# A two-layer sparse and forgetting attention trunk on one core: loads ordered by need, forget sums and function tables ahead of attention, the last two output units in halves of positions

## The chip, the cores and the metric

The kernel runs on one core of one Trainium2 chip. The metric is device time in microseconds (us) of one execution. All times come from runs on the chip, all stretches from one profiled execution.

## What is computed

The reference is a trunk of two layers over 512 positions of width 1024, in float32:

```
for l in range(DEPTH):                      # DEPTH = 2
    h = rms_norm(x, norm_g[l])
    proj = jnp.einsum('btd,dc->btc', h, w_in[l])
    q_a, kv_a, g_a, z_a, q_b, k_b, v_b, f_b, z_b, merge = jnp.split(proj, split_at, axis=-1)
    y_a = nsa_mixer(q_a, kv_a, g_a, cmp_pe_k[l], cmp_w1_k[l], cmp_w2_k[l],
                    cmp_pe_v[l], cmp_w1_v[l], cmp_w2_v[l], cos, sin) * jax.nn.silu(z_a)
    y_b = fox_mixer(q_b, k_b, v_b, f_b, b_forget[l]) * jax.nn.silu(z_b)
    r_a, r_b = jnp.split(merge, 2, axis=-1)
    merged = (jax.nn.sigmoid(r_a) * (y_a @ w_proj_nsa[l]) + jax.nn.sigmoid(r_b) * (y_b @ w_proj_fox[l]))
    x = x + merged @ w_out[l]
return rms_norm(x, final_g)
```

`nsa_mixer` has 16 heads in two groups. It compresses blocks of 32 keys and values (adds position vectors, a hidden layer with weights w1, silu, a second layer w2), attends to the compressed, the selected and the windowed keys with rotated queries and keys, and weighs the three by gates. `fox_mixer` is causal attention with a bias from the running sum over positions of log_sigmoid(f + b_forget), the forget sums.

## The kernel before

The program is written out engine by engine, with semaphores between them. Activations stand transposed: 1024 features as eight chunks of 128 partitions by 512 positions. Every projection is cut into *units* of 128 output columns. A unit is one load of weights (512 KB, `load` on SyncE's queue, into one of two buffers `w_raw`), a rounding into `w_hi` by ScalarE (`split_hi`), a rest `w_lo` by VectorE (`split_lo`), and 24 matmuls of 512 columns on TensorE (`unit_piece`, L1545: three for each of eight chunks). A load waits until `w_lo_done` says that its buffer has been split for the unit two before.

A layer has five stages.

- Prologue (first layer only): TensorE multiplies a constant tile 12 and 8 times (`run_in`), turns the eight chunks of x, ScalarE and VectorE copy them out and make `u_hi` and `u_lo`, and unit 0 follows chunk by chunk.
- Ten units of keys and values, `kv(0)` to `kv(9)`: 0 and 1 are the inputs of the compression (`c_raw`), 2 and 3 the gates and forget logits (narrow, 48 and 16 columns, multiplied together as `gf_w` on L1725 and L1726), the others keys, the first queries and values. Between them come `hidden(a)` (the compression's hidden layer for keys, a = 0, and values, a = 1), the rotation on GpSimd, the forget sums on VectorE (L1401, L1404, L1407, with an exponential and a logarithm on ScalarE), and turns of v.
- Eight cycles of attention, in which further units are spread between the steps of a `Plan`. Before the first one VectorE finishes `v_rest` and `z_silu_of`, and ScalarE `z_tanh_of`.
- The merge, and eight output units (`U_OUT`) with the residual sum.
- After the last layer: turns of the normed output, sums of squares, a root, a scaling by row and four stores of 512 KB.

What matters for the order: each engine runs its instructions strictly in the order in which they are written. Unit 4 uses the same accumulator `acc[0]` as unit 0, and may start once `c_raw` of unit 0 has been read, which VectorE does after `split_lo(*kv(4))`:

```
split_lo(*kv(4))
dve.wait_ge(rstd_spread, l + 1)
dve.tensor_copy(rstd[:, :], misc[:, :]).then_inc(rstd_done, 1)
dve.wait_ge(rstd_done, l + 1)
c_raw_of(0)
```

Of the kernel before, what the change touches and what calls it, by code (L numbers as in the profile page):

```python
# [143 lines left out]
def bass_trunk(nc, x, norm_g, w_in, b_forget, pe_k, w1_k, w2_k, pe_v, w1_v, w2_v, w_nsa, w_fox,  # L144
               w_out, final_g, rope_c, rope_s, out):
    ctx = ExitStack()
    with ctx:
# [177 lines left out]
        c_landed = sem("c_landed")  # L325
# [49 lines left out]
        o_t_done = sem("o_t_done")  # L375
        o_turned = sem("o_turned")
# [75 lines left out]
        def _(sp):  # L452
# [7 lines left out]
            def load_compression(l, n):  # L460

                for a, w1, w2, pe in ((0, w1_k, w2_k, pe_k), (1, w1_v, w2_v, pe_v))[n:n + 1]:
                    for j in (slice(0, CJ // 2), slice(CJ // 2, CJ)):
                        sp.dma_start(c_w1[:, a:a + 1, j, :],  # L464
                                     w1.rearrange("l (j p) h -> p l j h", p=P)[:, bass.ds(l, 1), j]
                                     ).then_inc(c_landed, 16)
                    sp.dma_start(c_w2[:, a:a + 1, :],
                                 w2.rearrange("l h d -> h l d")[:, bass.ds(l, 1)]).then_inc(c_landed, 16)
                    with nc.allow_non_contiguous_dma(reason="8 kB of position vectors, transposed"):
                        for par in range(2):  # L470
                            sp.dma_start(c_pe[HD * par:HD * par + HD, a:a + 1, :],
                                         pe.rearrange("l (j a) d -> a d l j", a=2)[par][:, bass.ds(l, 1)]
                                         ).then_inc(c_landed, 16)
# [41 lines left out]
            for qt in range(QT):  # L515
                sp.wait_ge(o_scaled[qt % 2], qt // 2 + 1)
                sp.dma_start(out[0, qt * P:(qt + 1) * P, :], o_nat[:, qt, :]).then_inc(o_stored, 16)
# [4 lines left out]
        def _(pool):  # L522
# [135 lines left out]
            pool.wait_ge(rope_landed, 32)  # L658
            for l in range(DEPTH):
# [8 lines left out]
                            0.0).then_inc(pads, 1)  # L668
                rotate(l, 0, q_raw)
# [28 lines left out]
        def _(act):  # L698
# [91 lines left out]
            def body(cycle):  # L790
# [55 lines left out]

                m = nsa.m
# [24 lines left out]
            table_of_sqrt()  # L872
            for to, src in ((cosT[:, :], rope_c), (sinT[:, :], rope_s)):
# [5 lines left out]
            split_hi(0, 0, wait=False)  # L879
            act.wait_ge(gains_done, 1)  # L880
            for k in range(KT):
                if k % 2:
                    act.wait_ge(x_turned, k + 1)
                    act.activation(xT[:, k, :], x_banks[k % 4][:, :], ACT.Copy).then_inc(x_odd, 1)
                    act.wait_ge(x_odd, k // 2 + 1)
                else:
                    act.wait_ge(x_done, k // 2 + 1)
                u_high(0, k)
# [6 lines left out]
            for l in range(DEPTH):  # L895
# [55 lines left out]
                q_round((0, 1), [(rope_done, l * 10 + 2)])  # L951
                act.wait_ge(f_exp, 3 * l + 1)
                act.activation(f_b[F_ROWS, :], f_b[F_ROWS, :], ACT.Ln, bias=1.0).then_inc(f_exp, 1)
                split_hi(*kv(8))
# [3 lines left out]
                act.wait_ge(f_step, 6 * l + 5)  # L958
                act.activation(f_hi[F_ROWS, :], f_b[F_ROWS, :], ACT.Copy).then_inc(f_exp, 1)
# [61 lines left out]
                for k in range(KT):  # L1021
                    if k < KT - 1 or l + 1 < DEPTH:
# [808 lines left out]
```

## Time and profile before

| | us |
|---|---|
| median of 3 runs | 1512.32 (1512.21 to 1512.59) |
| the profiled execution | 1511.46 |
| its span, first to last record | 1509.7 |
| TensorE matmuls busy | 1477.7 |
| VectorE, ScalarE, GpSimd busy | 1027.5, 906.2, 482.9 |
| mean granted clock of TensorE | 0.993 of full |

The profiled time is the span and 1.76 us around it, and lies 0.86 us under the median. TensorE is busy 98% of the span, so time can come only from where it stands idle or runs at its lower clock: between the start and the first cycle of each layer, and at the end.

### The profile page before, as it was taken

To read this page: it belongs to the slowest core of one execution; us is meant where nothing else is said; L and a number is where in the kernel's file an instruction comes from. 1 tells how busy PE (TensorE), PEld (TensorE's weight loads), DVE (VectorE), ACT (ScalarE), POOL (GpSimd) and SP (SyncE) were. 2 spreads that over 40 slices of the span, in tenths; PEclk is the share of its full clock that TensorE was granted. 3 is DMA by queue.
4 is the path that set the end of the run, shared out by engine and by line. 5 is a ranking of instruction groups with operands and counts; after the bars stand their busy time and mean duration, and the time that the engine had idled before them with its cause. 6 is when DMAs were issued, how large, how long until landed. Compare 5 with 4: busy or idle time off the path is not lost.

```text
span 1509.7 us, 24892 instructions
## 1 busy us (share of the span) xinstructions
PE 1477.7 (98%) x7645; PEld 1241.2 (82%) x7645; DVE 1027.5 (68%) x2455; ACT 906.2 (60%) x1883; POOL 482.9 (32%) x578
## 2 busy tenths in 40 slices
PE   7999999999999999999999999999999999999997
PEld 6878888888888888888877888888888888888886
DVE  4778788788788874434557788788788787643443
ACT  4667777777777762223445777777777776422233
POOL 1425445445455420000013445445355363000000
PEclk9999999999999999999999999999999999999999
DMA  9222222222122143332452212122222221433332
GB/s 247 69 73 57 56 57 56 56 53 61 46 52 62 51 125 98 93 102 84 127 148 73 67 47 61 51 57 57 57 57 56 56 57 47 149 89 106 86 96 84
DMA packets 221827, 117.86 MB, mean 78 GB/s; under 512 B 17560, under 2 KB 220336, under 8 KB 221232
## 3 DMA queue, kind: packets, MB, share of 16 engines
q1 hardware_dynamic: 219584, 107.66, 26.9%
q0 software_dynamic: 1728, 8.66, 1.6%
q8 instruction: 40, 0.66, 0.2%
q10 hardware_dynamic: 432, 0.54, 0.1%
q14 instruction: 43, 0.35, 0.1%
HBM read 110.41 MB, written 6.42 MB: 77 GB/s over the span
## 4 chain that ended last, share of the span: by engine, by line
PE 85%; DVE 6%; ACT 3%; issue 2%; POOL 1%; SPq 1%; DMA 1%; ACTq 0%; DVEq 0%; POOLq 0%
PE acc L1545 60%; PE o_pair L1623 7%; PE turned L1605 7%; PE scores L1597 4%; PE scores L1596 4%; ACT w_hi L704 1%; DVE w_lo L1044 1%; PE misc L1634 1%; DMA w_raw<-in_w_in_dram 1%; DVE kk_lo L1146 1%; DVE yt_lo L1429 1%; SPq L464 1%; PE misc L1568 1%; PE o_pair L1649 0%; PE scores L1679 0%
## 5 line engine op out<-in xcount | busy, mean ns | idle before, releaser
L1545 PE MATMUL acc<-u_hi,w_hi 128*128 128x512 f32 x1120 | 444.9, 397 | 11.5 <-DVE c_raw L1085 9.5
L1545 PE MATMUL acc<-u_lo,w_hi 128*128 128x512 f32 x1120 | 442.9, 395 | 0.0
L1545 PE MATMUL acc<-u_hi,w_lo 128*128 128x512 f32 x1120 | 442.7, 395 | 0.0
L820 ACT ACTIVATE prob<-prob,row_max 128x128 f32<-128x128 f32 (+3 forms) x384 | 215.1, 560 | 184.6 <-DVE row_max L1210 182.7
L1044 DVE TENSOR_TENSOR w_lo<-w_raw,w_hi 128x1024 fp32r<-128x1024 f32 x188 | 233.0, 1240 | 96.4 <-ACT w_hi L704 94.4
L631 POOL TENSOR_SCALAR prob<-prob,row_inv,gates 128x128 f32<-128x128 f32 (+3 forms) x256 | 169.9, 664 | 336.5 <-DVE row_inv L1217 332.4
L704 ACT ACTIVATE w_hi<-w_raw 128x1024 fp32r<-128x1024 f32 x188 | 197.9, 1053 | 104.9 <-PE acc L1545 86.6
L1545 PEld LDWEIGHTS acc<-u_hi,w_hi 128*128 128x128 f32 x1120 | 211.5, 189 | 54.5 <-issue 12.0
L1545 PEld LDWEIGHTS acc<-u_hi,w_lo 128*128 128x128 f32 x1120 | 211.6, 189 | 40.0
L1545 PEld LDWEIGHTS acc<-u_lo,w_hi 128*128 128x128 f32 x1120 | 211.6, 189 | 38.1
L1210 DVE CUSTOM_DVE_ANT_0 prob<-scores,causal 128x128 f32<-128x128 f32 (+3 forms) x384 | 184.9, 482 | 43.5 <-PE scores L1597 33.2
L829 ACT ACTIVATE pt_hi<-turned 128x128 fp32r<-128x128 f32 (+3 forms) x384 | 163.3, 425 | 44.8 <-PE turned L1605 42.8
L1222 DVE TENSOR_TENSOR pt_lo<-turned,pt_hi 128x128 fp32r<-128x128 f32 (+3 forms) x384 | 186.3, 485 | 3.4 <-ACT pt_hi L829 3.0
L628 POOL TENSOR_SCALAR prob<-prob,row_inv 128x128 f32<-128x128 f32 (+3 forms) x128 | 145.3, 1137 | 85.3 <-DVE row_inv L1217 84.9
L1605 PE MATMUL turned<-ident,prob 128*128 128x128 f32 x960 | 169.7, 275 | 2.9 <-POOL prob L628 1.1
L1605 PEld LDWEIGHTS turned<-ident,prob 128*128 128x128 f32 x960 | 117.1, 141 | 31.3 <-POOL prob L631 3.5
L1217 DVE RECIPROCAL row_inv<-row_sum 128x1 f32<-128x1 f32 x384 | 60.4, 157 | 76.5 <-ACT prob L820 73.5
L1596 PE MATMUL scores<-kk_hi,q_nsa 128*128 128x128 f32 (+3 forms) x256 | 100.4, 393 | 3.0 <-DVE row_max L1210 3.0
L1545 PE MATMUL acc<-yt_hi,w_hi 128*128 128x512 f32 x256 | 101.0, 395 | 0.6 <-DVE w_lo L1044 0.6
L1545 PE MATMUL acc<-yt_hi,w_lo 128*128 128x512 f32 x256 | 100.4, 392 | 0.0
L1545 PE MATMUL acc<-yt_lo,w_hi 128*128 128x512 f32 x256 | 99.5, 389 | 0.0
L1597 PE MATMUL scores<-kk_lo,q_nsa 128*128 128x128 f32 (+3 forms) x256 | 82.1, 321 | 0.0
(197 smaller groups left out, 2228.8 us busy)
## 6 DMA issues: line engine op xcount, KB each, us to landing
w_raw<-in_w_in_dram SPq DMA_DIRECT2D x140, 512.0 KB, 3.8
w_raw<-in_w_proj_nsa_dram SPq DMA_DIRECT2D x16, 512.0 KB, 3.9
w_raw<-in_w_proj_fox_dram SPq DMA_DIRECT2D x16, 512.0 KB, 4.1
w_raw<-in_w_out_dram SPq DMA_DIRECT2D x16, 512.0 KB, 4.1
x_scratch<-xT POOLq DMA_DIRECT2D x2, 2048.0 KB, 7.8
xT<-x_scratch POOLq DMA_DIRECT2D x2, 2048.0 KB, 8.6
x_nat<-in_x_dram SPq DMA_DIRECT2D x4, 512.0 KB, 8.1
c_w<-in_cmp_w_k_dram SPq DMA_DIRECT2D x4, 512.0 KB, 7.5
```

The lines of the kernel that those rows point to most:

```text
L628: ins = pool.tensor_scalar(p, p, row_inv[:, ring:ring + 1], None, ALU.mult)
L631: ins = pool.tensor_scalar(p, p, row_inv[:, ring:ring + 1], gate, ALU.mult, ALU.mult)
L704: act.activation(w_hi[:, par, :, 0:width], w_raw[:, par, :, 0:width], ACT.Copy).then_inc(w_hi_done, 1)
L820: act.activation(prob[:, ring, 0:width], prob[:, ring, 0:width], ACT.Exp, bias=row_max[:, ring:ring + 1], scale=-1.0, accum_out=row_sum[:, ...
L829: act.activation(pt_tiles(pt_hi, a, qt), turned_tiles(s, qt), ACT.Copy)\
L1044: dve.tensor_tensor(w_lo[:, par, :, 0:width], w_raw[:, par, :, 0:width], w_hi[:, par, :, 0:width], ALU.subtract).then_inc(w_lo_done, 1)
L1210: dve.tensor_tensor_reduce(prob[:, ring, 0:width], scores[s % 2][:, 0:width], causal[:, T - width:T], -SCALE, BIG, ALU.add, ALU.min, row_m ...
L1222: dve.tensor_tensor(pt_tiles(pt_lo, a, qt), turned_tiles(s, qt), pt_tiles(pt_hi, a, qt), ALU.subtract).then_inc(pt_lo_done, 1)
L1545: ins = pe.matmul(acc[par][0:width, :], w[:, par, k, 0:width], rhs, start=(n == 0), stop=(n == 23))
L1596: pe.matmul(to, q_hi, k_hi[:, 0:n], start=True, stop=False)
L1597: pe.matmul(to, q_with, k_lo[:, 0:n], start=False, stop=True).then_inc(s_mm, 1)
L1605: ins = pe.transpose(turned[s % 2][:, P * kt:P * kt + P], prob[:, s % SM_RING, P * kt:P * kt + P], ident[:, :])
```

## The change

Five things change.

- *Loads.* The compression's loads are cut in two (`load_hidden` for w1, `load_second` for w2 and the position vectors) with a semaphore for keys and one for values. Those for keys go behind units 2 and 3, those for values behind unit 5.
- *Prologue.* `run_in` does 8 and 4 times. ScalarE copies the odd chunk first and then makes `u_hi` of both, TensorE takes unit 0 by pairs of chunks, and ScalarE issues the loads of the rotation tables and biases behind the chunks.
- *Forget sums.* The logarithm goes ahead of the rounding of q on ScalarE, and the sums ahead of `q_rest` on VectorE.
- *Tables.* One element of Tanh is computed ahead of `v_round`, and `z_tanh_of`, `z_silu_of` and the second `v_rest` go into steps 1, 3 and 0 of the first cycle.
- *End.* Output units 6 and 7 are computed for positions 0 to 255 and then for 256 to 511, with squares, root, turn, scaling and stores by halves. The last of the four stores is issued by ScalarE.

```diff
+            def load_hidden(l, a, w1):
+                for j in (slice(0, CJ // 2), slice(CJ // 2, CJ)):
+                    sp.dma_start(c_w1[:, a:a + 1, j, :],
+                                 w1.rearrange("l (j p) h -> p l j h", p=P)[:, bass.ds(l, 1), j]
+                                 ).then_inc(c_landed[a], 16)
...
-                    if n in (1, 3):
-                        load_compression(l, n // 2)
+                    if n == 2:
+                        load_hidden(l, 0, w1_k)
+                    if n == 3:
+                        load_second(l, 0, w2_k, pe_k)
+                    if n == 5:
+                        load_hidden(l, 1, w1_v)
+                        load_second(l, 1, w2_v, pe_v)
...
+            for k in range(0, KT, 2):
+                act.wait_ge(x_turned, k + 2)
+                act.activation(xT[:, k + 1, :], x_banks[(k + 1) % 4][:, :], ACT.Copy).then_inc(x_odd, 1)
+                act.wait_ge(x_done, k // 2 + 1)
+                u_high(0, k)
+                act.wait_ge(x_odd, k // 2 + 1)
+                u_high(0, k + 1)
             for to, src in ((cosT[:, :], rope_c), (sinT[:, :], rope_s)):
                 act.dma_start(to, src).then_inc(rope_landed, 16)
...
+                act.wait_ge(z_done, 2 * PAIRS * l + 1)
+                act.activation(z_th[:, 0:1], ones[:, 0:1], ACT.Tanh)
                 act.wait_ge(x_saved, 16 * (l + 1))
                 v_round(l * 10, v_pair[:, :, 0, :, 0:HD])
                 v_round(l * 10 + 1, v_pair[:, :, 1, :, 0:HD])
-                z_tanh_of(2 * PAIRS * l, 0)
...
+                if cycle.first:
+                    at(0, lambda: v_rest(l * 10 + 1, v_pair[:, :, 1, :, HD:2 * HD], v_pair[:, :, 1, :, 0:HD]))
+                    at(3, lambda: z_silu_of(2 * PAIRS * l, 0))
...
+            last_piece(0, 0)
+            turn_out(KT - 4)
+            last_piece(0, 1)
+            turn_out(KT - 3)
+            last_piece(1, 0, 0, 14)
+            last_sums(0)
+            last_piece(1, 0, 14)
+            last_turns(0)
+            last_piece(1, 1)
+            last_sums(1)
+            last_turns(1)
```

SyncE's queue at the start of the program, before; `c_w` and `c_pe` are the compression's weights and position vectors, 128x8x128 of `w_raw` a full unit, 128x8x48 and 128x8x16 the narrow units 2 and 3:

```order
L457 DMA w_raw<-in_w_in_dram 128x8x128
L464 DMA c_w<-in_cmp_w_k_dram 128x8x128 x2
L467 DMA c_w<-in_cmp_w_k_dram 128x64
L471 DMA c_pe<-in_cmp_pe_k_dram 64x16x1 x2
L457 DMA w_raw<-in_w_in_dram 128x8x48
L457 DMA w_raw<-in_w_in_dram 128x8x16
L464 DMA c_w<-in_cmp_w_v_dram 128x8x128 x2
L467 DMA c_w<-in_cmp_w_v_dram 128x64
L471 DMA c_pe<-in_cmp_pe_v_dram 64x16x1 x2
L457 DMA w_raw<-in_w_in_dram 128x8x128 x6
```

The same queue with the change:

```order
L466 DMA w_raw<-in_w_in_dram 128x8x128
L466 DMA w_raw<-in_w_in_dram 128x8x48
L472 DMA c_w<-in_cmp_w_k_dram 128x8x128 x2
L466 DMA w_raw<-in_w_in_dram 128x8x16
L478 DMA c_w<-in_cmp_w_k_dram 128x64
L482 DMA c_pe<-in_cmp_pe_k_dram 64x16x1 x2
L466 DMA w_raw<-in_w_in_dram 128x8x128 x2
L472 DMA c_w<-in_cmp_w_v_dram 128x8x128 x2
L478 DMA c_w<-in_cmp_w_v_dram 128x64
L482 DMA c_pe<-in_cmp_pe_v_dram 64x16x1 x2
L466 DMA w_raw<-in_w_in_dram 128x8x128 x4
```

Between unit 3's load and unit 4's there stood the five loads for values; now there stand three small ones for keys, and the two halves of the keys' w1 stand ahead of unit 3's load.

VectorE before the first cycle, before, from the rest of the queries (L1121) to the first row maximum:

```order
L1121 TENSOR_TENSOR q_nsa<-q_rope,q_nsa 64x512 x2
L1085 TENSOR_TENSOR qk_raw<-acc,rstd 128x512
L1044 TENSOR_TENSOR w_lo<-w_raw,w_hi 128x1024
L1388 TENSOR_SCALAR kcb<-scores 64x2x32 x2
L1393 TENSOR_SCALAR vcb<-scores 32x2x64 x4
L1397 SCALAR_TENSOR_TENSOR vcb<-scores,vcb 32x2x64 x4
L1401 SCALAR_TENSOR_TENSOR f_a<-f_a,f_b 32x512
L1404 SCALAR_TENSOR_TENSOR f_b<-ones,f_a 32x512
L1407 TENSOR_SCALAR f_b<-f_b 32x512
L1085 TENSOR_TENSOR z_silu<-acc,rstd 128x512
```

The same place with the change, which begins three rows earlier:

```order
L1435 SCALAR_TENSOR_TENSOR f_a<-f_a,f_b 32x512
L1438 SCALAR_TENSOR_TENSOR f_b<-ones,f_a 32x512
L1441 TENSOR_SCALAR f_b<-f_b 32x512
L1170 TENSOR_TENSOR q_nsa<-q_rope,q_nsa 64x512 x2
L1134 TENSOR_TENSOR qk_raw<-acc,rstd 128x512
L1445 TENSOR_TENSOR f_lo<-f_b,f_hi 32x512
L1093 TENSOR_TENSOR w_lo<-w_raw,w_hi 128x1024
L1452 TENSOR_SCALAR kcb<-scores 64x2x32 x2
L1457 TENSOR_SCALAR vcb<-scores 32x2x64 x4
L1461 SCALAR_TENSOR_TENSOR vcb<-scores,vcb 32x2x64 x4
L1134 TENSOR_TENSOR z_silu<-acc,rstd 128x512
```

The three instructions of the forget sums now stand ahead of the rest of the queries, and their rest `f_lo` ahead of the split of unit 8.

## Rows read from the trace of the kernel before

**Rows 1.** The page, first part: TensorE's busy time, share and instructions.
```profile
PE 1477.7 (98%) x7645; PEld 1241.2 (82%) x7645; DVE 1027.5 (68%) x2455; ACT 906.2 (60%) x1883; POOL 482.9 (32%) x578
```

**Rows 2.** Who TensorE waited for, 0 to 92 us: total, times, longest.
```profile
PE acc L1545 <- DVE c_raw L1085: 6.2, 1, 6.2
...
PE scores L1596 <- DVE row_max L1210: 1.5, 1, 1.5
PE misc L1568 <- DVE z_silu L1085: 1.0, 1, 1.0
```

**Rows 3.** The same, 740 to 850 us; row_max reads as above.
```profile
PE acc L1545 <- DVE c_raw L1085: 3.3, 1, 3.3
...
PE misc L1568 <- DVE z_silu L1085: 0.6, 1, 0.6
```

**Rows 4.** Timeline of TensorE, first layer: start, duration, what, [idle before].
```profile
37.85 0.77 PE L1545 MATMUL acc<-u_hi,w_hi 128*128 128x512 f32 x1 [6.24 <-DVE c_raw L1085]
...
88.02 0.44 PE L1596 MATMUL scores<-kk_hi,q_nsa 128*128 128x384 f32 x1 [1.49 <-DVE row_max L1210]
```

**Rows 5.** Two-us windows of TensorE: length, busy, granted clock, DMA share, GB/s.
```profile
34.00:36.00 2.00, 0.00 (x0) 0.68 0.54 137
...
774.00:776.00 2.00, 0.00 (x0) 0.85 0.00 0
```

**Rows 6.** Timeline of SyncE's queue, first layer.
```profile
20.99 5.12 SPq L464 DMA_DIRECT2D c_w<-in_cmp_w_v_dram  x2
...
29.00 1.37 SPq L457 DMA_DIRECT2D w_raw<-in_w_in_dram  x1
```

**Rows 7.** Timeline of ScalarE and its queue, first layer.
```profile
3.60 0.47 ACTq L877 DMA_DIRECT2D b_f<-in_b_forget_dram  x1
...
18.20 1.04 ACT L704 ACTIVATE w_hi<-w_raw 128x1024 fp32r<-128x1024 f32 x1
...
34.06 1.06 ACT L704 ACTIVATE w_hi<-w_raw 128x1024 fp32r<-128x1024 f32 x1 [6.83 <-DMA w_raw<-in_w_in_dram]
...
63.92 1.27 ACT L743 ACTIVATE q_nsa<-q_rope 64x512 fp32r<-64x512 f32 x2 [4.04 <-POOL q_rope L569]
65.21 1.28 ACT L953 ACT_TABLE_LOAD   x1
...
85.11 1.28 ACT L783 ACT_TABLE_LOAD   x1
```

**Rows 8.** Timeline of VectorE, first layer.
```profile
24.99 0.55 DVE L1314 TENSOR_TENSOR gf_w<-w_raw,gf_w 128x384 fp32r<-128x384 f32 x1
...
35.15 1.23 DVE L1044 TENSOR_TENSOR w_lo<-w_raw,w_hi 128x1024 fp32r<-128x1024 f32 x1 [7.59 <-ACT w_hi L704]
...
72.83 1.38 DVE L1401 SCALAR_TENSOR_TENSOR f_a<-f_a,f_b 32x512 f32<-32x512 f32 x1
...
75.94 0.69 DVE L1085 TENSOR_TENSOR z_silu<-acc,rstd 128x512 f32<-128x512 f32 x1
```

**Rows 9.** The chain that ended last, pieces in order: start, duration, what.
```profile
1.73 5.49 PE scores L1679 x24
...
767.32 5.43 DMA w_raw<-in_w_in_dram
...
776.62 8.36 PE acc L1545 x24
...
841.54 1.22 PE o_pair L1623 x8
...
1492.45 5.51 PE acc L1545 x24
```

**Rows 10.** SyncE's stores at the end, timeline.
```profile
1502.78 2.90 SPq L517 DMA_DIRECT2D out_dram<-o_nat  x4
```

**Rows 11.** DMA, 1503 to 1509.7 us: GB/s in 40 slices.
```profile
GB/s 0 0 0 147 391 416 391 391 391 391 416 391 416 440 367 416 440 391 391 392 391 416 391 416 416 391 391 392 440 465 416 391 416 367 245 0 0 0 0 0
```

More of the change, by code:

```diff
@@ new lines, in last_piece @@
+            def last_piece(h, p):
+                cols = T_HALF[h]
+                act.wait_ge(last_x, 2 * h + p + 1)
+                act.wait_ge(sq_added, (KT - 2) * (DEPTH - 1) + KT - 4 + p)
+                act.activation(squares[:, p, cols], xT[:, KT - 2 + p, cols], ACT.Square).then_inc(last_sq, 1)
+                act.wait_ge(o_turned, KT - 3 + p)
+                act.activation(o_t[:, p, cols], xT[:, KT - 2 + p, cols], ACT.Copy, scale=gain(DEPTH, KT - 2 + p)
+                               ).then_inc(last_o_t, 1)
@@ L1685, in _ @@
                          ).then_inc(gains_turned, 1)
-            run_in(8)
-            for k in range(KT + 4):
+            run_in(4)
+            for k in range(KT + 2):
                 if k < KT:
@@ L1787, in turn_out @@
                     ins.then_inc(o_turned, 1)
-                for k in range(KT):
+                for k in range(KT if l + 1 < DEPTH else KT - 2):
                     unit_piece(0, 24, half0 + U_OUT // 2 + k // 2, k % 2, hi=m_hi, lo=m_lo,
@@ L1794, in _, with last_piece @@
                         turn_out(k - 2)
-            turn_out(KT - 2)
-            sum_squares(DEPTH)
-            turn_out(KT - 1)
+            def last_piece(h, p, first=0, last=24):
+                half, cols = half0 + U_OUT // 2 + KT // 2 - 1, T_HALF[h]
+                for n in range(first, last):
+                    k, which = divmod(n, 3)
+                    if n == 0 and h == 0:
+                        pe.wait_ge(w_lo_done, 2 * half + p + 3)
+                        pe.wait_ge(x_done, X_EVEN + KT * (DEPTH - 1) + KT - 3 + p)
+                    elif n == 0:
+                        pe.wait_ge(last_x, p + 1)
+                    ins = pe.matmul(acc[p][:, cols], (w_lo if which == 2 else w_hi)[:, p, k, :],
+                                    (m_lo if which == 1 else m_hi)[:, k, cols], start=(n == 0), stop=(n == 23))
+                    if n == 23:
+                        ins.then_inc(last_mm, 1)
@@ new lines, in last_sums @@
+            def last_sums(h):
+                pe.wait_ge(last_added, h + 1)
+                pe.wait_ge(var_done, DEPTH + h)
+                for qt in (2 * h, 2 * h + 1):
+                    pe.matmul(misc[:, qt:qt + 1], sq_sum[:, P * qt:P * qt + P], ones[:, 0:1],
+                              start=(qt == 2 * h), stop=False, skip_group_check=True)
+                pe.wait_ge(last_sq, 2 * h + 2)
+                for qt in (2 * h, 2 * h + 1):
+                    ins = pe.matmul(misc[:, qt:qt + 1], squares[:, 1, P * qt:P * qt + P], ones[:, 0:1],
+                                    start=False, stop=(qt == 2 * h + 1), skip_group_check=True)
+                ins.then_inc(last_summed, 1)
@@ new lines, in last_turns @@
+            def last_turns(h):
+                pe.wait_ge(last_o_t, 2 * h + 2)
+                for n in range(2):
+                    qt, bank = 2 * h + n, (scores, turned)[h][n]
+                    if h:
+                        pe.wait_ge(o_copied[n], KT // 2 - 1)
+                    for p in range(2):
+                        ins = pe.transpose(bank[:, P * p:P * p + P], o_t[:, p, P * qt:P * qt + P], ident[:, :])
+                ins.then_inc(last_turned, 1)
+            last_piece(0, 0)
```

206 lines of the change are left out of this document (127 added, 79 removed).

## The prediction, made before the changed kernel ran

> **What bounds the kernel now.** I read the page first. TensorE is busy 98% of the span [rows 1], so a faster VectorE or ScalarE is worth only what TensorE waits for them. Next I read who TensorE waited for, once for each layer's ten units. In the first layer one wait of 6.2 us stands out, for the `c_raw` that frees the accumulator of unit 4; behind it come 1.5 us for the first row maxima and 1.0 us for the value that is turned [rows 2]. The second layer has the same three: 3.3 and 0.6 us [rows 3], and the same 1.5 us for row maxima, in a row that reads like the first layer's [rows 2]. The timeline shows where the long one lies: unit 4 starts at 37.85, so TensorE stopped at 31.6 [rows 4]. Third, the clock. In the window 34 to 36 the granted clock is 0.68, and before and after it stands at one of two levels, full or half (2.4 or 1.2 GHz); 0.68 means 1.28 us at half, so it fell at about 34.7, 3.1 us after the matmuls stopped. In the second layer 0.85 puts the fall at 775.4, 2.1 us after they stopped at 773.3 [rows 3, 5]. The 24 matmuls of unit 4 then took 8.36 us, where a unit at full clock takes 5.51 [rows 9], so the wait costs another 2.85 us there.
>
> Who makes TensorE wait? The load of unit 4 is issued at 29.00, lands for ScalarE at 34.06, and the split on VectorE (35.15), the copy of rstd and the read of `c_raw` lead to 37.85 [rows 4, 6 to 8]. From landing to unit 4 that is 3.8 us. The load's own condition, the split of unit 2 on VectorE, was met at 24.99 + 0.55 = 25.54 [rows 8]. The 3.46 us between are SyncE's issues: from 20.99 it issued the two halves of w1 for values, 5.12 us, and the small loads behind them until 29.00, 2.9 us [rows 6]. In the second layer the same load is issued at 767.32 and needs 5.43 us [rows 9].
>
> **Loads.** With the change only the small loads, 2.9 us, stand between the loads of units 3 and 4. They end near 23.9, and the split at 25.5 decides. If that split keeps its time, unit 4's load goes out 3.46 us earlier and unit 4 starts at 37.85 - 3.46 = 34.4. Transfer kept at the 5.06 us of rows 6 and 7 (29.00 to 34.06). In the second layer up to 5.1 us of issues are gone and 3.3 us of idle can be had; all of it is taken, since the chain only has to move 3.3 us. What is late next: unit 5's load follows directly; the w1 halves for values come out some 7 us later than before, between units 5 and 6. Behind a wait for them on VectorE stand `blocks(1)`, the split of unit 6 and the gates. With 5.12 us of issue from about 28.5 and a landing like unit 4's they are there at about 39, and the work that wants them stands behind the start of unit 4 plus its 5.5 us. So this is free, and starts to cost beyond about 42.
>
> **Prologue.** 24 records of the warm-up took 5.49 us [rows 9], 0.229 each. The first group loses 8 of them, 1.8 us, so the chunks may start up to 1.8 us earlier, if x has landed. Against that ScalarE now issues four loads ahead of the rounding of unit 1, which started at 18.20: one such issue took 0.47 [rows 7], four 1.9 us. Net zero, with bounds -1.8 and +1.9 us.
>
> **The clock.** First layer: idle shrinks from 6.24 to 2.8 us. The falls seen came 3.1 and 2.1 us after the stop, so this gap lies between them. I take half of the 2.85 us as regained, 1.4; bounds 0 and 2.85. Second layer: the gap closes, all 2.85 comes back.
>
> **Forget sums and tables.** On VectorE the sums fill 72.83 to 75.94, 3.1 us [rows 8], ahead of the value that TensorE waited 1.0 us for. In their new place VectorE and ScalarE had a hole: ScalarE waited 4.04 us for the rotated q before L743 [rows 7], and table load and logarithm fit in (1.28 plus an activation). The Tanh table (85.11, 1.28 us [rows 7]), z_tanh and z_silu stood ahead of the first row maximum, for which TensorE waited 1.5 us. VectorE's chain thus moves earlier by 3.5 + 3.1 + at least 1.3 = 7.9 us, more than the 3.5 + 2.5 that TensorE can use at the same clock. So the gain is the waits: 1.5 + 1.0 = 2.5 us in the first layer, 2.1 in the second. Bounds: nothing, if other waits take their place, and the same 2.5 and 2.1, since no more is there. The extra rest, tanh and silu inside the first cycle are three instructions of about 0.7 us; VectorE is busy 68% overall [rows 1], and I cost them at nothing. With no cover they cost up to 2 us a layer.
>
> A rule speaks against this. The row shows a table load of 1.28 us that follows the activation before it at once, since L743 ends at 65.19 and the load starts at 65.21 [rows 7]. The Trainium skill, page "ScalarE: Activation LUTs", section "What ACT_TABLE_LOAD costs", counts some 1.38 us of draining on top, 2.66 us a switch. By that the new Tanh switch ahead of `v_round` would come 1.4 us later a layer, and the sum would be up to 2.8 us less. This trace shows no such drain.
>
> **The end.** Two units by halves: eight matmuls with 2 x (512 + 384 + 256 + 128) = 2560 columns took 1.22 us [rows 9], so one of 256 columns takes 0.122, and 96 of them 11.7 against 2 x 5.51: +0.7. Before, the last unit ended at 1497.96 [rows 9] and the first store was issued at 1502.78 [rows 10], 4.8 us later. The data then flowed at about 400 GB/s from 1503.5 to 1508.8 [rows 11], 5.3 us for 2.1 MB: the four stores are bound by what the transfers carry, not by their issues of 0.73 each. With the change only two stores, 1.05 MB, are left for the end: 2.65 us. TensorE's last piece ends at about 1500.4 (0.7 later for the halves, and an estimated 1.7 for the first half's turns and sums that now stand ahead of it). The rest of the path has half the columns; I take 3.1 of the 4.8 us. Issue at 1503.5, plus 0.73, 2.65 and the 0.9 between the last data and the span's end: 1507.8 against 1509.7, -1.9 us. Bounds: +0.7 if the turns and sums hide nothing, and -3.3.
>
> **The sum.** First layer 3.5 + 1.4 + 2.5 = 7.4, second 3.3 + 2.85 + 2.1 = 8.25, end 1.9: 17.5 us. The span becomes 1492.2, the profiled execution (1.76 around the span) 1493.9, and the median, which lies 0.86 above that execution, 1494.8.
>
> **Rivals.**
> - *All of the clock.* The first layer's gap closes further, because the chunks start earlier and the issues on ScalarE cost less than 1.9 us; then 1.4 to 3.2 us more come back: 1492. For it: the bounds of the prologue. Against: the transfer of 5 us and the 3.8 us behind it stay.
> - *New waits.* In the ten units VectorE is next: with TensorE 3 us earlier at full clock, it waits for `c_blk` ahead of `hidden(0)` or for `w_lo` of unit 8. For it: both layers' VectorE chain has few holes there. Price about 2 to 3 us a layer: 1499.5.
> - *The load comes no earlier.* Unit 4's load is issued at 25.5 but lands near 34, since transfers for x and the tables fill the engines. Then 3.5 + 1.4 and 3.3 + 2.85 are lost, and 6.4 us of gain stay: 1506. Against: the transfers' share was free for some of that time.
> - *The drain of the rule above:* 1497.6.
> - *Slower.* One mechanism: the values' w1, now behind unit 5's load, lands so late that VectorE stands before `blocks(1)`. Its slack is 42 - 39 = 3 us, after which each us costs one. It would have to land beyond 39 + 3 + 17.5 = 59.5 to make the kernel slower; the transfers of rows 6, 7 and 9 took 5 us.
>
> **Chances.** Forecast 60% (1492.5 to 1497), all of the clock 13%, new waits 15%, no earlier load 6%, drain 4%, slower or no change 2%. The range 1490.5 to 1501 leaves out the late load and the last one. Within 0.2%, 3 us, a measurement of this kernel can't tell from no change. Faster 0.97, same 0.02, slower 0.01.
>
> **What would show it.** Right: TensorE's wait for `c_raw` at 3 us or less in the first layer and under 1 in the second; granted clock full from 770 on; the waits for row maxima and z_silu gone from the list; matmuls of 256 columns 0.12 us apart; data of the last stores flowing 2.6 us. Wrong: unit 4's load landing after 32 us, unit 4 of the second layer at 8 us again, new entries `PE <- c_blk` or `PE <- w_lo` of over 1 us, or the first cycle longer than before by the moved tanh and silu.

## The result: 13.0 us faster, of 17.5 forecast

| | median, us | range |
|---|---|---|
| before, on the same chip | 1512.26 | 1512.08 to 1512.59 |
| changed | 1499.26 | 1498.7 to 1500.25 |

Each row is of four runs. The ratio is 0.9917, with a 95% interval of 0.9906 to 0.9929. The forecast was 1494.8 (1490.5 to 1501.0): the direction and the range held. The 4.5 us that are missing bring the time to the number of the rival "new waits", 1499.5. That closeness is in part luck: the new wait costs more in each layer than the rival's 2 to 3 us, and small waits that nobody had counted went away. The profiled execution of the changed kernel took 1498.70 us, its span 1497.0.

The page of the changed kernel, first part, answers to [rows 1]:

```profile
PE 1473.5 (98%) x7677; PEld 1241.3 (83%) x7677; DVE 1029.9 (69%) x2461; ACT 907.5 (61%) x1891; POOL 486.3 (32%) x578
```

TensorE's share has hardly moved, and says nothing here. Who TensorE waited for, changed kernel, 0 to 92 us (total, times, longest), answers to [rows 2]:

```profile
PE acc L1635 <- DVE c_raw L1134: 3.2, 1, 3.2
PE acc L1635 <- DVE w_lo L1093: 2.3, 1, 2.3
PE scores L1769 <- POOL ident L542: 1.7, 1, 1.7
PE acc L1635 <- DVE u_lo L1111: 1.6, 4, 0.7
PE acc L1635 <- issue: 1.2, 1, 1.2
```

The wait for `c_raw` is 3.2 us instead of 6.2, and the waits for row maxima and z_silu are gone. In their place stands one for `w_lo`, of unit 8: one of the entries that the prediction had named as a sign of being wrong. In the second layer it is the only wait that the view lists; it takes the place of [rows 3]. The next view is 740 to 850 us:

```profile
PE acc L1635 <- DVE w_lo L1093: 2.0, 1, 2.0
```

The timeline of TensorE in the first layer (start, duration, what, idle before) answers to [rows 4]:

```profile
35.22 0.47 PE L1635 MATMUL acc<-u_hi,w_hi 128*128 128x512 f32 x1 [3.15 <-DVE c_raw L1134]
...
68.15 0.80 PE L1635 MATMUL acc<-u_hi,w_hi 128*128 128x512 f32 x1 [2.33 <-DVE w_lo L1093]
...
83.63 0.34 PE L1686 MATMUL scores<-kk_hi,q_nsa 128*128 128x384 f32 x1
```

And in windows of 2 us (length, busy, granted clock, DMA share, GB/s), answering to [rows 5]:

```profile
34.00:36.00 2.00, 0.79 (x4) 1.00 1.23 244
...
66.00:68.00 2.00, 0.00 (x0) 0.97 0.00 0
68.00:70.00 2.00, 1.85 (x4) 0.50 0.22 35
70.00:72.00 2.00, 2.00 (x7) 0.67 0.76 227
...
800.00:802.00 2.00, 0.70 (x3) 0.94 0.00 0
802.00:804.00 2.00, 2.00 (x6) 0.50 0.71 173
```

Before unit 4 the clock did not fall in this execution. Before unit 8 it did, in both layers, to half (1.2 GHz); the prediction had wanted it full from 770 us on. The chain of the changed kernel shows the price (start, duration, what), to be read beside a unit at full clock, 5.51 in [rows 9]:

```profile
65.92 2.18 DVE w_lo L1093
68.15 7.23 PE acc L1635 x24
...
799.06 2.19 DVE w_lo L1093
801.30 7.33 PE acc L1635 x24
```

So unit 8 costs 2.3 + 1.7 us in the first layer and 2.0 + 1.8 in the second.

**Where the time went.** The span falls into four sections, bounded by the first score product of 384 columns in each layer and by the begin of the second layer (its sum of squares on TensorE). Each row is worked out from the timelines of one profiled execution, in us:

| kernel | to the first cycle | layer 1 behind it | layer 2 to its first cycle | rest |
|---|---|---|---|---|
| before | 88.02 | 673.28 | 65.92 | 682.48 |
| forecast | 80.6 | 673.3 | 57.7 | 680.6 |
| changed | 83.63 | 673.26 | 59.99 | 680.12 |
| split8_first | 82.08 | 673.37 | 57.10 | 680.25 |
| frest_late | 81.33 | 673.32 | 57.57 | 680.18 |
| forget_back | 83.16 | 673.75 | 59.86 | 680.13 |
| loads_back | 85.12 | 673.30 | 61.95 | 680.23 |
| tables_back | 84.24 | 673.41 | 62.07 | 680.48 |
| prologue_back | 81.21 | 673.26 | 60.10 | 680.13 |
| split8_second_late | 81.28 | 673.27 | 56.72 | 680.13 |
| rope_late | 83.68 | 673.34 | 60.54 | 680.34 |
| end_back | 83.49 | 673.24 | 59.47 | 682.40 |
| loads_alone | 83.75 | 673.34 | 62.03 | 682.38 |
| best2 | 79.80 | 673.18 | 56.71 | 680.21 |
| best2_busy | 79.20 | 673.19 | 56.68 | 680.23 |

The reader sees that the second column does not move: the tanh, silu and rest that went into the first cycle cost nothing. The end gave 2.4 us, 0.5 more than forecast. The first layer gave 4.4 us instead of 7.4, the second 5.9 instead of 8.25. These two sections are what the experiments are about.

### The profile page after: what moved, and what is told of

Same layout as the page of the kernel before. It is cut to its first block, busy times and chain, and to the rows that moved or that the text cites. A ratio compares the mean times of both kernels' runs of the same rounds, so it can differ in the third digit from the quotient of the medians.

```text
span 1497.0 us, 24977 instructions
## 1 busy us (share of the span) xinstructions
PE 1473.5 (98%) x7677; PEld 1241.3 (83%) x7677; DVE 1029.9 (69%) x2461; ACT 907.5 (61%) x1891; POOL 486.3 (32%) x578
## 4 chain that ended last, share of the span: by engine, by line
PE 87%; DVE 5%; ACT 4%; issue 2%; POOL 1%; SPq 1%; DMA 1%; ACTq 0%; DVEq 0%; POOLq 0%
PE acc L1635 61%; PE o_pair L1713 7%; PE turned L1695 7%; PE scores L1687 4%; PE scores L1686 4%; ACT w_hi L720 1%; DVE w_lo L1093 1%; PE misc L1724 1%; PE acc L1896 1%; ACT q_swap L750 1%; DMA w_raw<-in_w_in_dram 1%; DVE yt_lo L1479 1%; PE misc L1658 1%; PE o_pair L1739 0%; PE misc L1732 0%
```

## Experiments

The kernel before was timed again beside the experiments: 1511.79 with the first four, 1511.99 with the next four, 1512.07 with the last four. The changed kernel was not, so that its 1499.26 is compared across 0.2 to 0.5 us of drift. Behind each measured time stands its ratio to the kernel before, with its interval. An interval of a ratio is about 0.0015 to each side, 2.3 us, so differences between two variants of less than that rest on their profiles more than on their medians.

**1. Unit 8's split first.** Both splits of unit 8, and the read of unit 6 that frees its accumulator, go ahead of the forget sums and the rounding of the rotated q.

```diff
                 act.activation(f_b[F_ROWS, :], f_b[F_ROWS, :], ACT.Ln, bias=1.0).then_inc(f_exp, 1)
+                split_hi(*kv(8))
                 q_round((0, 1), [(rope_done, l * 10 + 2)])
...
                 act.activation(f_hi[F_ROWS, :], f_b[F_ROWS, :], ACT.Copy).then_inc(f_exp, 1)
-                split_hi(*kv(8))
...
                 hidden(1)
+                raw_of(*kv(6), l * 10 + 2, [], to=qk_raw)
+                split_lo(*kv(8))
                 dve.wait_ge(f_exp, 3 * l + 2)
...
                 q_rest(l * 26 + 1)
-                raw_of(*kv(6), l * 10 + 2, [], to=qk_raw)
...
-                split_lo(*kv(8))
```

> The changed kernel (1499.3 us), but in both layers the two splits of unit 8 and the read of unit 6 stand ahead of the rounding and the rest of the rotated queries and of the forget sums. Theory A (TensorE now runs ahead of the rotation chain, and unit 8's split, written behind the rotated queries, is the new wait): TensorE's waits for w_lo of 2.3 and 2.0 us fall below 0.5, the stretch at half clock behind them goes, 2.8 + 3.1 us come back: about 1493.5. Theory B (the forget sums' and their rest's new place is the cause, by 2.9 us of extra work ahead of that split): also about 1493.5; the next kernel tells them apart. Theory C (the wait would move to the next unit): within 1 us of 1499.3.

Measured 1493.67 (0.9878, 0.9861 to 0.9894): 5.6 us back, by moving two splits. The wait of unit 8 is gone in both layers (0.3 us stand ahead of unit 9 in the second); clock full from 66 to 74 and from 796 to 804 us. In the second layer the section is 57.10, 0.6 under what I had forecast. The first stays 1.5 above: unit 4 starts at 35.55, not at 34.4, and here the clock fell in its gap. In the changed kernel VectorE's row of this split took 2.17 us, and here (timeline of split8_first) it is:

```profile
62.67 1.23 DVE L1093 TENSOR_TENSOR w_lo<-w_raw,w_hi 128x1024 fp32r<-128x1024 f32 x1 [0.46 <-ACT w_hi L720]
```

**2. Forget sums in their old place.** Logarithm, sums, `f_hi` and `f_lo` as before, all else changed.

```diff
+                q_round((0, 1), [(rope_done, l * 10 + 2)])
                 act.wait_ge(f_exp, 3 * l + 1)
                 act.activation(f_b[F_ROWS, :], f_b[F_ROWS, :], ACT.Ln, bias=1.0).then_inc(f_exp, 1)
-                q_round((0, 1), [(rope_done, l * 10 + 2)])
-                act.wait_ge(f_step, 6 * l + 5)
-                act.activation(f_hi[F_ROWS, :], f_b[F_ROWS, :], ACT.Copy).then_inc(f_exp, 1)
                 split_hi(*kv(8))
...
-                dve.tensor_tensor_scan(f_b[F_ROWS, :], ones[F_ROWS, 0:1].broadcast_to([GF // 2, T]), f_a[F_ROWS, :], 0.0,
...
+                dve.tensor_tensor_scan(f_b[F_ROWS, :], ones[F_ROWS, 0:1].broadcast_to([GF // 2, T]), f_a[F_ROWS, :], 0.0,
...
                 v_of(*kv(7), z_silu[:, 0, :], [])
```

> The changed kernel with the forget sums, their logarithm and their rest back in the old places, all else as changed. Theory A: the split of unit 8 still stands behind the rotated queries and the logarithm; it would end 2.4 us earlier than in the kernel before (69.9), at about 67.5, so TensorE still waits 1.7 to 2 us for it in each layer, and the old wait of 0.5 to 1 us for the values comes back: 1499 to 1502. Theory B: the wait for unit 8 is gone (under 0.5 us) and the time falls by 2 to 5 us, to 1494 to 1497.

Measured 1498.54 (0.9913, 0.9896 to 0.9929), 0.7 below the changed kernel and 0.5 below theory A's range: as the change moves them, with their rests, the sums are worth nothing. The z_silu wait of 1.1 us comes back in each layer. The wait of unit 8 goes in the first layer, where TensorE comes later by the clock that fell at unit 4, and shrinks to 1.5 us in the second; 0.4 us of `w_lo` stand ahead of unit 9 in both, as in the kernel before. What one end gains the other pays. Experiment 6 shows that this is not so of the sums alone.

**3. Loads in their old order.**

```diff
-                    if n == 2:
-                        load_hidden(l, 0, w1_k)
-                    if n == 3:
+                    if n == 1:
+                        load_hidden(l, 0, w1_k)
                         load_second(l, 0, w2_k, pe_k)
-                    if n == 5:
+                    if n == 3:
                         load_hidden(l, 1, w1_v)
                         load_second(l, 1, w2_v, pe_v)
```

> The changed kernel with the compression's loads back behind units 1 and 3, all else as changed. Theory A: unit 4 of the first layer starts near 37.9 again after a wait of some 6 us and at half clock, in the second layer a wait of 3.3 us and half clock, worth 4.3 and 6.2 us; but then the wait for unit 8 (2.8 and 3.1 us) is not there, since TensorE no longer runs ahead: +4.5 us net, 1503 to 1505. If the loads and the wait at unit 8 had nothing to do with each other: +10.5 us, 1510.

Measured 1503.56 (0.9948, 0.9932 to 0.9965), in theory A's range: the loads are worth 4.3 us inside the whole change. The waits for `c_raw` are 6.2 and 3.0 again; the one for unit 8 is gone in the first layer and 0.8 us in the second.

**4. Tables in their old place.**

```diff
-                act.wait_ge(z_done, 2 * PAIRS * l + 1)
-                act.activation(z_th[:, 0:1], ones[:, 0:1], ACT.Tanh)
...
+                z_tanh_of(2 * PAIRS * l, 0)
...
-                    at(0, lambda: v_rest(l * 10 + 1, v_pair[:, :, 1, :, HD:2 * HD], v_pair[:, :, 1, :, 0:HD]))
-                    at(3, lambda: z_silu_of(2 * PAIRS * l, 0))
...
+                v_rest(l * 10 + 1, v_pair[:, :, 1, :, HD:2 * HD], v_pair[:, :, 1, :, 0:HD])
+                z_silu_of(2 * PAIRS * l, 0)
```

> The changed kernel with the Tanh table, the tanh, the silu and the second rest of v back ahead of the first cycle. By my prediction the row maxima come later by the table load of 1.28 us and three instructions of 0.7, so TensorE waits about 2 us for them again in each layer: 1502.5 to 1504. Rival (other work of that place hides it): within 1 us of 1499.3. By the extra drain that the Trainium skill counts for a table load, 1.4 us more a layer: 1505.5 to 1507.

Measured 1501.90 (0.9933, 0.9916 to 0.9950): 2.6 us slower, 0.6 less than my prediction's range for it, with the 1.5 us for row maxima back in both layers. Nothing was lost to a drain. In the changed kernel the load of a table for the logarithm starts at once behind the activation that ends at 57.26, and the one for the moved Tanh behind the split that ends at 76.54 (timeline of ScalarE):

```profile
57.03 0.23 ACT L930 ACTIVATE c_th<-turned 128x64 f32<-128x64 f32 x1
57.28 1.28 ACT L970 ACT_TABLE_LOAD   x1
58.57 0.63 ACT L970 ACTIVATE f_b<-f_b 32x512 f32<-32x512 f32 x1
...
76.56 1.28 ACT L980 ACT_TABLE_LOAD   x1
77.85 0.20 ACT L980 ACTIVATE z_th<-ones 128x1 f32<-128x1 f32 x1
```

**5. Prologue of before.** 12 and 8 warm-up products, unit 0 by single chunks, ScalarE's four loads ahead of them.

```diff
-            run_in(8)
+            run_in(12)
...
-            run_in(4)
+            run_in(8)
-            for k in range(KT + 2):
+            for k in range(KT + 4):
...
-                if k % 2 and k > 1:
-                    unit_piece(3 * (k - 3), 3 * (k - 1), 0, 0,
+                if k >= 4:
+                    unit_piece(3 * (k - 4), 3 * (k - 3), 0, 0,
```

> The changed kernel with the prologue of before (12 and 8 warm-up products, unit 0 chunk by chunk, ScalarE's four loads ahead of the chunks). Theory A: the changed prologue saved 8 warm-up products and lost as much to the later rounding of unit 1, so that it is worth nothing or costs 0.5 us: unit 1 starts at 20.6 instead of 21.17, and the time is 1498.7 to 1499.5. Rival: the eight warm-up products were 1.8 us of pure gain and the rest of the program is late for other reasons: then 1501.

Measured 1495.79 (0.9891, 0.9875 to 0.9906): 3.5 us faster than the changed kernel by the medians, 2.4 us by the first section of the profiles. Both theories missed. The gates' section begins at 27.23 instead of 28.06, so 0.83 us of it is direct in this profile. (The three others with this prologue and the new order of loads, loads_alone, best2 and best2_busy, begin it at 26.24 to 26.45, so the direct part may be larger.) The rest is at unit 8: its wait in the first layer is 0.7 us, and the clock stays full. TensorE's row of unit 4 and VectorE's of unit 8's split with this prologue, to be read beside those of the changed kernel (35.22 above, and 65.92 under experiment 6):

```profile
34.27 0.69 PE L1635 MATMUL acc<-u_hi,w_hi 128*128 128x512 f32 x1 [3.04 <-DVE c_raw L1135]
...
64.97 2.21 DVE L1094 TENSOR_TENSOR w_lo<-w_raw,w_hi 128x1024 fp32r<-128x1024 f32 x1
```

Unit 4 starts 0.95 us earlier, and so does VectorE's split of unit 8; but here the clock fell in unit 4's gap, so that TensorE reaches `hidden(0)` 0.65 us later (41.43, not 40.78). 0.95 + 0.65 = 1.6 is what the wait lost, from 2.3 to 0.7, and with it the fall of the clock at unit 8.

**6. The rests of the forget sums late.** Only `f_hi` and `f_lo`, 0.6 and 0.7 us, go behind the splits.

```diff
                 q_round((0, 1), [(rope_done, l * 10 + 2)])
+                split_hi(*kv(8))
...
                 act.activation(f_hi[F_ROWS, :], f_b[F_ROWS, :], ACT.Copy).then_inc(f_exp, 1)
-                split_hi(*kv(8))
...
                 raw_of(*kv(6), l * 10 + 2, [], to=qk_raw)
+                split_lo(*kv(8))
...
                 dve.tensor_tensor(f_lo[F_ROWS, :], f_b[F_ROWS, :], f_hi[F_ROWS, :], ALU.subtract).then_inc(f_step, 1)
-                split_lo(*kv(8))
```

> The changed kernel with only the rounding f_hi and the rest f_lo of the forget sums behind the two splits of unit 8; the sums themselves stay ahead. Theory A (whatever stands ahead of the two splits of unit 8 is paid on TensorE, with the clock on top): the split ends some 0.9 us earlier, the wait for w_lo of unit 8 falls from 2.3 and 2.0 to 1.4 and 1.1 us, and with less of the clock lost the time is 1496 to 1498. Rival (the wait is set by the rotated q alone, and what stands behind it is free): 1499.

Measured 1493.69 (0.9878, 0.9863 to 0.9893): 5.6 us for two small instructions a layer (4.6 by the profiled executions), as much as experiment 1, and more than theory A allowed. Unit 8 waits no longer in the first layer and 0.6 us in the second. Two timelines show why. The changed kernel, VectorE and GpSimd:

```profile
65.21 0.68 DVE L1445 TENSOR_TENSOR f_lo<-f_b,f_hi 32x512 fp32r<-32x512 f32 x1
65.92 2.17 DVE L1093 TENSOR_TENSOR w_lo<-w_raw,w_hi 128x1024 fp32r<-128x1024 f32 x1
...
65.38 1.63 POOL L579 TENSOR_TENSOR q_rope<-qk_raw,cosT 128x512 f32<-128x512 f32 x1 [3.87 <-DVE qk_raw L1134]
```

frest_late:

```profile
65.42 1.22 DVE L1093 TENSOR_TENSOR w_lo<-w_raw,w_hi 128x1024 fp32r<-128x1024 f32 x1
66.67 1.67 DVE L1446 TENSOR_TENSOR f_lo<-f_b,f_hi 32x512 fp32r<-32x512 f32 x1
...
65.71 2.08 POOL L579 TENSOR_TENSOR q_rope<-qk_raw,cosT 128x512 f32<-128x512 f32 x1 [3.87 <-DVE qk_raw L1134]
```

In the first, GpSimd starts at 65.38 and ends at 67.01; the split starts at 65.92 and ends at 68.09, 1.08 us behind GpSimd's end, so it stood for about 1 us. In the second the split starts first and takes its 1.22 us, and GpSimd stands: its row ends at 67.79, 1.15 us behind the split's end. Whoever starts first runs, the other waits for its end. (POOL's durations are rough; the ends agree with this reading to 0.15 us.) The Trainium skill, page "SBUF — State Buffer", section "SBUF: two separate sides", says just this of a VectorE instruction with two inputs in SBUF beside a GpSimd instruction that reads SBUF: the pair of ports is held for the whole instruction. The trace agrees. So `f_lo` cost the split its own 0.7 us and the lost race of another 0.95. In the kernel before, GpSimd had started first as well, but 0.7 us ahead of the split (68.25, shown below), and the race cost 0.4:

```profile
67.54 1.29 POOL L563 TENSOR_TENSOR q_rope<-qk_raw,cosT 128x512 f32<-128x512 f32 x1 [3.65 <-DVE qk_raw L1085]
```

Read together, experiments 2 and 6 part the sums from their rests. In both the rests stand behind unit 8's splits, and only in this one the logarithm and the sums stand ahead of them: 1493.69 against 1498.54. The sums alone are worth 4.9 us; `f_hi` and `f_lo` ahead of the splits took that back.

**7. The keys' small loads behind unit 4's.** On top of experiment 1.

```diff
-                    if n == 3:
+                    if n == 4:
                         load_second(l, 0, w2_k, pe_k)
```

> The kernel of split8_first (1493.67) with the keys' w2 and position vectors loaded behind unit 4's weights and not ahead of them. Theory A (their 5.0 us on SyncE, where I had counted 2.9, hold unit 4's load back to 26.67): unit 4's load is issued at 25.5 to 26, unit 4 starts 0.7 to 1.2 us earlier in the first layer and nothing changes in the second: 1492.5 to 1493. Rival (the issues only move on and hold back unit 5's load, which then waits as long): 1493.7 or more, with a wait in unit 5.

Measured 1492.92 (0.9875, 0.9860 to 0.9891): 0.75 us less than experiment 1, as expected, though medians alone could not tell so little; the profiles put it at 0.8 in the first layer and 0.4 in the second. The wait for `c_raw` is 2.2 us, and no wait stands in the second layer. What these loads took on SyncE is the first fence, of the changed kernel; the second is of this one:

```profile
21.55 1.51 SPq L478 DMA_DIRECT2D c_w<-in_cmp_w_k_dram  x1
23.11 3.46 SPq L482 DMA_DIRECT2D c_pe<-in_cmp_pe_k_dram  x2
26.67 1.78 SPq L466 DMA_DIRECT2D w_raw<-in_w_in_dram  x2
```

```profile
27.18 0.57 SPq L478 DMA_DIRECT2D c_w<-in_cmp_w_k_dram  x1
27.80 1.44 SPq L482 DMA_DIRECT2D c_pe<-in_cmp_pe_k_dram  x2
```

5.0 us ahead of unit 4's load, 2.0 behind it. The halves of w1 are not what stretches the issue: in the changed kernel they were issued from 8.59 to 13.02 and had landed by 18.0. What was under way from 21.55 on was GpSimd's store of `xT`, issued at 17.48 and landed at 25.6, and the narrow load of unit 3, landed at 27.3 (view of DMA, changed kernel, 7 to 36 us; the last number is from issue to landing):

```profile
x_scratch<-xT POOLq DMA_DIRECT2D x1, 2048.0 KB, 8.1
c_w<-in_cmp_w_k_dram SPq DMA_DIRECT2D x2, 512.0 KB, 7.2
```

In experiment 7 the store had landed at 26.2, before the small loads were issued. Which of the two transfers holds the issue up was not separated.

**8. The end of before.** The last two units over all positions, four stores by SyncE.

> The changed kernel with the end of before: units 6 and 7 of the last layer over all 512 positions, four stores by SyncE behind everything. Theory A (the trace's tail of 21.07 us against 23.2 is this part alone): 1501.4, and the span from the start of unit 6 to the end is 23.2 us again. Rival (part of the tail's gain is one of the clock or of other work): 1500.3 or less.

Measured 1500.33 (0.9920, 0.9906 to 0.9933), 1.1 us slower by the medians, 2.3 by the section's profiles (682.40 against 680.12). The median alone would have favoured the rival; its interval holds both. The section is the better witness, since nothing else in it differs.

**9. ScalarE's four loads later.** Behind the rounding of unit 1 and the squares, the prologue else as changed.

```diff
                 u_high(0, k + 1)
-            for to, src in ((cosT[:, :], rope_c), (sinT[:, :], rope_s)):
-                act.dma_start(to, src).then_inc(rope_landed, 16)
...
             split_hi(0, 1, wait=False)
...
                                accum_out=squared[:, qt:qt + 1]).then_inc(sq_summed, 1)
+            for to, src in ((cosT[:, :], rope_c), (sinT[:, :], rope_s)):
+                act.dma_start(to, src).then_inc(rope_landed, 16)
```

> The changed kernel with ScalarE's four loads (rotation tables and biases) behind the rounding of unit 1 and the four squares, not ahead of them; the prologue stays by pairs of chunks. Theory P (the prologue of the change costs because unit 1's rounding waits 0.68 us for those issues): unit 1 starts at 20.5 instead of 21.17, the gates' section some 0.6 us earlier, and the time is 0.7 to 2.5 us less than that of the changed kernel: 1496.5 to 1498.5. Rival (the loss lies in the pairs: ScalarE waits 1.02 us for a pair of turned chunks): 1499.

Measured 1498.11 (0.9911, 0.9898 to 0.9925), 1.1 us less, within theory P's range; but its profile does not carry that theory: TensorE waits 1.8 us for `gf_w`, since the narrow load of unit 3 landed 1.3 us later (28.70), and SyncE's `c_pe` took 5.18 us. ScalarE's wait of 1.0 us for a pair of turned chunks stands in this profile as in that of the changed kernel (16.26, 1.02 us), and not in the one of experiment 5. The issues and the pairs both have a part in the 0.83 us, and three profiles part them. The first turn of x on TensorE and the rounding of unit 1 on ScalarE, for the changed kernel, prologue_back and rope_late in this order:

```profile
7.04 1.10 PE L1783 MATMUL turned<-ident,x_nat 128*128 128x128 f32 x8
18.75 1.06 ACT L720 ACTIVATE w_hi<-w_raw 128x1024 fp32r<-128x1024 f32 x1 [0.68 <-issue]
...
9.18 1.04 PE L1783 MATMUL turned<-ident,x_nat 128*128 128x128 f32 x8
18.11 1.04 ACT L720 ACTIVATE w_hi<-w_raw 128x1024 fp32r<-128x1024 f32 x1
...
7.54 1.17 PE L1783 MATMUL turned<-ident,x_nat 128*128 128x128 f32 x8
18.56 1.04 ACT L720 ACTIVATE w_hi<-w_raw 128x1024 fp32r<-128x1024 f32 x1
```

From the first turn to that rounding it is 11.7 us in the changed kernel, 11.0 with the issues later and 8.9 with the prologue of before. So the issues cost 0.7 us and the new order of the chunks, pairs with the odd one first, about 2.1, of which at most 0.4 is a wait for x that the changed kernel has there. The shorter warm-up starts the turns 2.1 us earlier and pays for most of it.

**10. All three together** (best2: experiments 1, 5 and 7).

> The changed kernel with unit 8's splits first, the keys' small loads behind unit 4's, and the prologue of before. If the three gains add up (5.6 + 0.8 + 3.5): 1489.5. They should not add in full, since the prologue's 3.5 us came for the greater part out of unit 8's wait and its clock, which the first edit takes already: theory A expects only the 0.83 us of the earlier start of the gates' section: 1492. The numbers tell the two apart.

Measured 1491.75 (0.9867, 0.9851 to 0.9882), 7.5 us under the changed kernel and 20.3 under the one before. The gains do not add: 1492 was the figure of theory A, 1489.5 the sum.

**11. The gap kept busy.** best2 with eight products of a constant tile ahead of unit 4, first layer only.

```diff
+                if l == 0:
+                    run_in(8)
                 kv(4)
```

> best2 with eight products of a constant tile (2.05 us at full clock) on TensorE in the first layer's gap ahead of unit 4. If the fall of the clock in this gap costs what the profiles show (unit 4 took 5.56 us in the changed kernel and 6.9 to 7.2 where it fell), this is 1.3 to 1.6 us faster than best2. If the timed executions mostly keep the clock in this gap, it is the same; if the products hold unit 4 back, slower by under 0.5.

Measured 1491.46 (0.9867, 0.9852 to 0.9883): 0.3 us, no difference. The clock did what it should, full from 32 to 40 us where best2 has 0.72 and 0.50. TensorE was then at `hidden(0)` at 38.97 instead of 39.90 and met the next wait there (view of waits, best2_busy, 0 to 92 us):

```profile
PE turned L1803 <- DVE c_blk L1388: 0.8, 1, 0.8
PE acc L1635 <- DVE w_lo L1094: 0.6, 1, 0.6
PE acc L1635 <- DVE c_raw L1135: 0.5, 1, 0.5
```

Of the 0.93 us two thirds (0.6) reach the first cycle in its profile. A clock regained ahead of a VectorE that has no hole is handed on as a wait.

**12. The loads alone**, on the kernel before.

> The kernel before with the ordered loads alone. Theory A (the loads give the wait for c_raw and, in the second layer, the clock; new waits for unit 8 take little because forget sums are not ahead of its split): 2.6 + up to 1.4 in the first layer and 3.3 + 2.85 in the second less what unit 8's wait takes: 1503 to 1506. If the 4.3 us by which loads_back was slower is all that they are worth anywhere: 1507.5. My prediction's terms for loads and clock, 3.5 + 1.4 + 3.3 + 2.85, would give 1501.

Measured 1503.48 (0.9945, 0.9931 to 0.9959): 8.6 us of gain, in theory A's range. From the begin of the second layer to `hidden(0)` this kernel takes 17.41 us, where the one before took 23.52: 6.1 us, my terms 3.3 + 2.85. Then a new wait of 1.5 us ahead of unit 8, at full clock, takes part of it back, and the wait for z_silu grows by 0.4: 3.9 us reach the first cycle. So the new wait does not need the forget sums in their new place; an earlier TensorE is enough for 1.5 us of it.

## Why the prediction was right, and which term was mis-sized

**Loads.** Right in direction, and in the second layer in size: with the clock, 6.15 us were forecast, 6.2 came. In the first layer unit 4 starts 2.63 us earlier, not 3.46. Two steps were off. One is "only the small loads, 2.9 us [...] end near 23.9": they were issued from 21.55 to 26.57, 5.0 us (experiment 7), where I had priced them by the ones for values. The load of unit 4 went out at 26.67, 0.6 us after its own condition was met, at 25.53 + 0.55 (timeline of VectorE, changed kernel):

```profile
25.53 0.55 DVE L1366 TENSOR_TENSOR gf_w<-w_raw,gf_w 128x384 fp32r<-128x384 f32 x1
```

The other is "if that split keeps its time": that condition was met 0.54 us later than before, by the prologue. A landing 0.3 us quicker gave some back: 3.46 - 0.6 - 0.54 + 0.3 = 2.6. With the prologue of before unit 4 starts at 34.27 (prologue_back) and 33.58 (loads_alone), 3.6 and 4.3 us earlier than 37.85 (in the second the turns of x start 1.1 us earlier, in the first as before), so the loads by themselves bring what was forecast for them.

**Clock at unit 4.** 1.4 forecast, 1.7 in this profile (unit 4 took 5.56 us instead of 7.27). The closeness is luck: the forecast took half of 2.85, the price of the second layer, where the first layer's own price was 1.7 and all of it came back. And of the eleven profiles in which this gap is 2.2 to 3.3 us the clock fell in seven and stood in four, those of end_back and of the changed kernel among them. Experiment 11 shows that it hardly matters.

**Forget sums and tables.** This is the term that failed: 2.5 and 2.1 us forecast, about 0 and -0.3 gained, which is what the loads and the clock leave of each section. The old waits did go (1.5 + 1.0 and 1.5 + 0.6, and two of 0.3 and 0.4 besides), and unit 8's wait with its clock, 4.0 and 3.8 us, came instead. The sentence that was wrong is "VectorE's chain thus moves earlier by 3.5 + 3.1 + at least 1.3 = 7.9 us". What moved earlier by that much is the chain's end, not its middle, where unit 8's split stands. In the kernel before, that split and the unit that takes it touch (timelines of VectorE and TensorE, before):

```profile
68.25 1.66 DVE L1044 TENSOR_TENSOR w_lo<-w_raw,w_hi 128x1024 fp32r<-128x1024 f32 x1 [0.92 <-ACT w_hi L704]
...
70.03 0.44 PE L1545 MATMUL acc<-u_hi,w_hi 128*128 128x512 f32 x1
```

It ended at 69.91 and was taken at 70.03. With the change it ends at 68.09, 1.8 us earlier, while TensorE is 4.4 us earlier (59.48 instead of 63.84 at the compression's second layer): 2.5 us, less 0.1 of slack, is the wait of 2.3.

Why only 1.8: from `c_raw` on VectorE has next to no idle time (0.19 us) until its gates, so that its `q_raw` moves as unit 4's start does (42.67, 2.65 us earlier), and not by the 1.7 us that TensorE regained from the clock. Of the 2.65 another 0.8 went to what was moved: the sums end at 63.04, and the rest of q behind them starts at 63.07, 2.15 us earlier than before and not 2.65; and the split lasts 0.5 us longer than the 1.66 before, less 0.2, the part of the hole of 0.92 that `f_lo` does not fill.

I named this rival, and gave it 15% and 2 to 3 us a layer; it had better evidence than that. VectorE does stand idle between `c_raw` and unit 8 in the kernel before, 5.0 us ahead of the rest of q, but there it waits for ScalarE, which waits for GpSimd (the 4.04 us of [rows 7]), which had waited for VectorE: the chain through the three engines has little slack, and its place in the order was known. That experiments 1 and 6 bring the second layer to 57.1 and 57.6 us against a forecast of 57.7 leaves no room for another large term there. Of the wait of 2.0 us in the second layer 1.5 stands even without the sums ahead of the split (experiments 2 and 12); with the sums ahead and their rests behind it, it is 0.6 (experiment 6). The step that failed is thus the 7.9 us of lead for the whole of VectorE's chain, and within it the place of `f_hi` and `f_lo`, which the prediction costed at nothing.

**Prologue.** Net zero forecast, with bounds of -1.8 and +1.9 us; the direct part is a loss of 0.83 us, within them. The terms were other ones: the turns start 2.2 us earlier than before (7.04 against 9.27), the four issues cost 0.7 and not 1.9, and the pairs, which the prediction did not cost at all, take 2.1 (experiment 9). What it set off downstream, another 1.6 us in the profile and more in the median, I had not seen: I costed the place where an engine starts and not who arrives late because of it.

**Tables' drain.** The rival of 1497.6 falls: no drain in any profile, and tables worth 2.6 us (experiment 4) against 3.0 us of row-maximum waits. The Trainium skill, page "ScalarE: Activation LUTs", section "What ACT_TABLE_LOAD costs", counts some 1.38 us of drain a switch, which would leave them an estimated 0.2. The trace does not bear it out: all eight loads of a table in the changed kernel take 1.28 us and start 0.02 us behind the activation before them.

**End.** -1.9 forecast, -2.4 by the sections. The last two units end 13.4 us after the first of them starts, where 11.5 was the figure before and 13.9 forecast. The stores at the end, changed kernel, 1485 to 1497 us (GB/s in 40 slices), answer to [rows 11]:

```profile
GB/s 0 0 0 0 0 0 0 0 0 0 0 96 410 382 396 423 396 410 423 382 178 0 0 0 0 0 0 0 341 410 437 396 369 410 396 396 341 0 0 0
```

Two bursts, of which only the second, nine slices of 0.3 us = 2.7 us, stands at the end: 2.65 was forecast.

## What to carry to other kernels

When TensorE is made earlier, ask of every engine that feeds it whether it becomes earlier by the same amount: a chain without a hole moves only by what moved its first link, and the difference comes back as a wait, with the clock's price on top. Before moving an instruction ahead of a split that TensorE waits for, check what GpSimd starts at that moment; two instructions of 0.6 and 0.7 us a layer in the wrong place cost 5.6 us here. And undo every part of a bundle once, and a part that comes out at nothing by pieces: this one held a part worth 8.6 us, one whose halves cancelled, and one that cost 2.4 to 3.5.

## What the runs showed of the hardware

- VectorE and GpSimd take turns: a split of 1.22 us took 2.17 when GpSimd had started first, and GpSimd's 1.29 us took 2.08 when VectorE had (experiment 6).
- The same gap of TensorE, 2.0 to 2.4 us ahead of unit 8, let the clock fall to half in some profiles and not in others: in end_back it fell in the first layer (0.94 and then 0.50) and not in the second; in rope_late the other way round. There and at unit 4, behind gaps of 2.0 to 3.0 us, a fall cost 1.3 to 1.8 us; behind the 3.3 us of the second layer before it cost 2.85. A clock that falls in one profile is thus no property of the kernel.
- The issue of the same two transposed loads of position vectors took from 1.44 us to 5.18 us on SyncE. The 5.18 us (rope_late) and the 3.46 us (changed kernel) fell while a store of 2 MB and a narrow load were under way, the 1.44 us behind the store.
